# Expert weights in a ring of 16 places, loads of two places from the fifth expert on, put-back products in two groups of eight

## The reference

```python
def hier_moe(x, w_grp, b_grp, w_rt, b_rt, w_gate, w_up, w_down):
    ...
    gate = (one_hot(g_idx)[:, :, None] * within[:, None, :]).reshape(T, N_EXPERTS)
    h = silu(einsum("td,edf->tef", xt, w_gate)) * einsum("td,edf->tef", xt, w_up)
    y = einsum("tef,efd->td", h * gate[:, :, None], w_down)

def reference(...):
    h = x
    h = h + pool_mixer(rmsnorm(h, norm_mix[0]), pool_w[0], pool_scale[0])
    h = h + hier_moe(rmsnorm(h, norm_ffn[0]), ...)            # layer 0
    k, v = shared_kv(h, kv_norm, w_kv, k_norm)
    h = h + stick_breaking_layer(rmsnorm(h, norm_mix[1]), k, v, w_q[0], q_norm[0], w_o[0])
    return h + hier_moe(rmsnorm(h, norm_ffn[1]), ...)         # layer 1
```

## Time and profile before

| | us |
|---|---|
| Median of three runs | 1383.72 |
| The three runs | 1380.75, 1383.72, 1383.76 |
| The profiled execution, its time | 1382.63 |
| Its span (first to last instruction) | 1380.7 |
| PE busy | 1336.4 (97%) |
| DVE busy, ACT busy | 557.0 (40%), 412.3 (30%) |
| DMA moved | 480.86 MB, mean 348 GB/s |

### The profile page before, as it was taken

How to read it: one execution, slowest core, us unless ns; L and a number is a source line. 1 busy time by engine, 2 the same in 40 slices (tenths; PEclk the granted TensorE clock), 3 DMA queues, 4 the chain that set the end, 5 groups by cost and what they waited for, 6 DMA issues and landing times.

```text
span 1380.7 us, 21741 instructions
## 1 busy us (share of the span) xinstructions
PE 1336.4 (97%) x9081; PEld 761.2 (55%) x9081; DVE 557.0 (40%) x906; ACT 412.3 (30%) x636; POOL 45.6 (3%) x37
## 2 busy tenths in 40 slices
PE   9899999998999999999999999999999999899998
PEld 8544444443344458888888887764434444334443
DVE  5813223232222246666665665561323223122223
ACT  5611111110111136665656575541111111011112
POOL 2200000000000000000000000110000000000000
PEclk9999999999999999999999999999999999999999
DMA  9999999999999999654535545579999999999997
GB/s 358 420 412 421 420 420 421 425 427 428 428 426 425 421 393 374 196 165 160 182 125 189 173 152 183 182 279 376 420 421 420 422 425 426 429 428 427 424 421 287
DMA packets 86223, 480.86 MB, mean 348 GB/s; under 512 B 6402, under 2 KB 6612, under 8 KB 46972
## 3 DMA queue, kind: packets, MB, share of 16 engines
q1 hardware_dynamic: 85708, 476.98, 86.1%
q10 hardware_dynamic: 432, 2.65, 0.5%
HBM read 477.51 MB, written 2.10 MB: 347 GB/s over the span
## 4 chain that ended last, share of the span: by engine, by line
issue 53%; PE 35%; DMA 7%; DVE 2%; POOL 1%; ACT 1%; SPq 1%; POOLq 0%; DVEq 0%; ACTq 0%
PE ps L1833 12%; PE ps L1641 8%; DMA ring<-in_moe_w_up 6%; PE ps L1871 5%; PE ps L1722 2%; PE ps L1887 2%; PE ps L1798 1%; PE ps L1799 1%; POOL head_rs L669 1%; DMA bias_row<-in_moe_b_rt 1%; PE ps L1926 1%; PE ps L1860 0%; DVE ws L1068 0%; PE ps L1662 0%; PE ps L1939 0%
## 5 line engine op out<-in xcount | busy, mean ns | idle before, releaser
L1833 PE MATMUL ps<-ring,xg 128*64 128x512 f32 x1536 | 361.1, 600 | 24.6 <-DMA ring<-in_moe_w_up 19.4
L1641 PE MATMUL ps<-ws,xs 128*128 128x512 f32 x1632 | 382.2, 392 | 2.5 <-DVE ws L1071 1.1
L1641 PEld LDWEIGHTS ps<-ws,xs 128*128 128x128 f32 x1632 | 302.9, 188 | 70.4 <-DVE ws L1071 3.6
L1833 PEld LDWEIGHTS ps<-ring,xg 128*64 128x64 f32 x1536 | 115.1, 138 | 238.0 <-issue 237.7
L1871 PE MATMUL ps<-ring,hidT 128*64 128x512 f32 x800 | 177.3, 595 | 0.0
L1071 DVE SCALAR_TENSOR_TENSOR ws<-ring,vecs,ws 128x512 fp32r<-128x512 f32 x192 | 134.3, 747 | 87.5 <-ACT ws L690 87.5
L1265 DVE TENSOR_TENSOR y_lo<-ps,y_hi 64x512 fp32r<-64x512 f32 x112 | 77.1, 689 | 191.6 <-ACT y_hi L754 188.9
L690 ACT ACTIVATE ws<-ring,vecs 128x512 fp32r<-128x512 f32 x192 | 127.3, 716 | 83.2 <-PE ps L1641 83.1
L745 ACT ACTIVATE silu_g<-ps,slot_scale 64x512 f32<-64x512 f32 x28 | 19.1, 683 | 401.1 <-PE ps L1833 401.1
L1245 DVE TENSOR_TENSOR resid<-resid,ps 128x512 f32<-128x512 f32 x112 | 72.0, 684 | 165.0 <-PE ps L1799 165.0
L754 ACT ACTIVATE y_hi<-ps 64x512 fp32r<-64x512 f32 x112 | 66.2, 591 | 209.2 <-PE ps L1871 207.2
(11 more groups left out here) (201 smaller groups left out, 865.0 us busy)
## 6 DMA issues: line engine op xcount, KB each, us to landing
ring<-in_moe_w_down SPq DMA_DIRECT2D x68, 1024.0 KB, 16.6
ring<-in_moe_w_gate SPq DMA_DIRECT2D x64, 1024.0 KB, 15.9
ring<-in_moe_w_up SPq DMA_DIRECT2D x64, 1024.0 KB, 16.4
ring<-in_moe_w_gate SPq DMA_DIRECT2D x24, 2048.0 KB, 16.4
ring<-in_moe_w_up SPq DMA_DIRECT2D x24, 2048.0 KB, 20.6
ring<-in_moe_w_down SPq DMA_DIRECT2D x24, 2048.0 KB, 19.3
ring<-in_w_kv SPq DMA_DIRECT2D x32, 1024.0 KB, 5.4
ring<-in_w_q SPq DMA_DIRECT2D x16, 1024.0 KB, 5.2
```

The source lines that it names most:

```text
L1641: last = mm(ps[:, bank + t, :], xs[:, px, k, cols], ws[:, b, pw, j, :], start=(first and j == 0 and n == 0), stop=(last_unit and j == 1 an ...
L1833: last = mm(ps[CAP * h:CAP * h + CAP, b, :], xg[:, b, k, :], both[h][:, j, :], start=(k == 0), stop=(k == KD - 1))
```

## The change

- **Places.** Four `outer` places (the memory of four of the five `extra`) join the 12 of the ring, and all blocks go round these 16 to the end of the layer. The fifth extra, `spare`, is used for two blocks (block 11 of expert 0 and block 4 of expert 2), and the two early places once, as before. `stage_places` works out the place of each load and the value of `slot_read` from which it is free.
- **Loads.** Experts 0 to 3 are loaded block by block, and from expert 4 on a load carries two blocks. This takes in gate and up of experts 14 and 15 and down of 14; down of 15 stays in four column blocks. Where gate and up come in two-block loads, one load holds the gate weights of quarters 0 and 1, one the up weights of the same quarters. So the PE waits for both ahead of quarter 0 and for the other two ahead of quarter 2.
- **Release.** A load of two waits until both places are read. Blocks are reported read after quarter 1 (four) and quarter 3 (four).
- **Puts.** The four puts m = 0 to 3 (eight products) stand behind the second quarter and m = 4 to 7 behind the third. They write banks 2 to 5 in turn, m waits for addition m - 3, and the first put waits for all four low parts of the pair before. The down products of the even expert wait for six of the additions, because they write banks 2 and 3.
- **Loops.** PE's pairs 2 to 5 are a loop of two rounds with two pairs in each; SP's experts 4 to 11 are a loop of two rounds with four experts in each.

```diff
-PAIR_SLOTS = 2 * SLOTS
-EXTRA = 5
-EARLY = 2
-WIDE = SLOTS + EXTRA
-PEELED = 3
-AHEAD = PEELED * PAIR_SLOTS
...
+LOADS = SLOTS * EXP
+OUTER = 4
+SINGLES = 4
+SPARE, EARLY = SLOTS + OUTER, SLOTS + OUTER + 1
+LAST = EXP - 1
+ROUND = [[*range(4, SLOTS), *range(4), *range(SLOTS, SLOTS + OUTER)], [*range(8, SLOTS), *range(8), *range(SLOTS, SLOTS + OUTER)]]
+ONCE = {("one", 0, 6): EARLY, ("one", 0, 7): EARLY + 1, ("one", 0, 11): SPARE, ("one", 2, 4): SPARE}
+STAGE = ([("one", e, m) for e in range(SINGLES) for m in range(SLOTS)]
+         + [("two", e, m) for e in range(SINGLES, LAST - 1) for m in range(6)]
+         + [("two", e, m) for e in (LAST - 1, LAST) for m in range(4)]
+         + [("two", LAST - 1, m) for m in (4, 5)] + [("col", LAST, c) for c in range(NBLK)])
+def read_at(load):
+    kind, e, m = load
+    if kind == "one":
+        return SLOTS * e + (2 * (m // 2) + 2 if m < 8 else m + 1)
+    if kind == "col":
+        return LOADS - NBLK + m + 1
+    if e < LAST - 1:
+        return SLOTS * e + (4, 4, 8, 8, 10, 12)[m]
+    return SLOTS * (LAST - 1) + (8 if e == LAST or m > 3 else 0) + (4, 4, 8, 8, 10, 12)[m]
+def stage_places(l):
+    place_of, free_at, holds, at = {}, {}, {}, 0
+    for load in STAGE:
+        if load in ONCE:
+            taken = [ONCE[load]]
+        else:
+            n = 2 if load[0] == "two" else 1
+            taken, at = [ROUND[l][(at + j) % len(ROUND[l])] for j in range(n)], at + n
+        free_at[load] = max(holds.get(p, 0) for p in taken)
+        place_of[load] = taken[0]
+        for p in taken:
+            holds[p] = read_at(load)
+    return place_of, free_at, holds
...
-        extra = at(32 * KB, "extra", [P, EXTRA, 2048])
-        early = [at(16 * KB * j, f"early{j}", [P, 2048]) for j in range(EARLY)]
+        outer = at(32 * KB, "outer", [P, OUTER, 2048])
+        spare = at(64 * KB, "spare", [P, 2048])
+        early = [at(16 * KB * j, f"early{j}", [P, 2048]) for j in range(2)]
...
+        def DOUBLE_FREE(e, m):
+            return SLOTS * (e - 2) + (10, 12, 16, 16, 20, 20)[m]
...
-                        nc.vector.tensor_tensor(rb, rb, ps[:, 4 + t, :], ALU.add).then_inc(resid_added, 1)
+                        nc.vector.tensor_tensor(rb, rb, ps[:, 2 + m % 4, :], ALU.add).then_inc(resid_added, 1)
...
+                def doubles(e0, i=0):
+                    for e in range(e0, e0 + 4):
+                        for m in range(6):
+                            sp.wait_ge(slot_read, LOADS * l + DOUBLE_FREE(e, m) + SLOTS * 4 * i)
+                            expert_load(l, ("two", e, m), e + 4 * i)
+                with sp.Fori(0, 2) as i:
+                    doubles(SINGLES, i)
+                for one in STAGE[SLOTS * SINGLES + 6 * 8:]:
+                    sp.wait_ge(slot_read, LOADS * l + FREE_AT[l][one])
+                    expert_load(l, one, one[1])
...
+                def gate_up(e, q, s=None):
+                    if e < SINGLES:
+                        return [one_at(loaded(("one", e, 2 * q + h))).rearrange("p (k c) -> p k c", k=4) for h in range(2)]
+                    both = [("two", e, 2 * (q // 2) + h) for h in range(2)]
+                    if q % 2 == 0:
+                        for two in both:
+                            loaded(two, s)
+                    return [two_at(PLACE_OF[l][two]).rearrange("p a (j f) -> p (a j) f", j=4)[:, 4 * (q % 2):4 * (q % 2) + 4, :]
+                            for two in both]
+                def blocks_read(e, q):
+                    return 2 if e < SINGLES else 4 * (q % 2)
+                def down_weights(e, k, s=None):
+                    if e < SINGLES:
+                        return one_at(loaded(("one", e, 8 + k)))
+                    two = ("two", e, 4 + k // 2)
+                    if k % 2 == 0:
+                        loaded(two, s)
+                    return two_at(PLACE_OF[l][two])[:, k % 2, :]
...
-                    if t == 0:
-                        pe.wait_ge(y_lo_done, NBLK * ((EXP + 1) * l + 2 * i + 1) + c + 1)
-                    pe.wait_ge(resid_added, add0 + 8 * i + m - 1)
-                    mm(ps[:, 4 + t, :], putT[:, t * P:(t + 1) * P], y_hi[:, c, :], start=True, stop=False)
-                    mm(ps[:, 4 + t, :], putT[:, t * P:(t + 1) * P], y_lo[c], start=False, stop=True).then_inc(mix_done, 1)
+                    if m == 0:
+                        pe.wait_ge(y_lo_done, NBLK * ((EXP + 1) * l + 2 * i + 1) + NBLK)
+                    pe.wait_ge(resid_added, add0 + 8 * i + m - 3)
+                    mm(ps[:, 2 + m % 4, :], putT[:, t * P:(t + 1) * P], y_hi[:, c, :], start=True, stop=False)
+                    mm(ps[:, 2 + m % 4, :], putT[:, t * P:(t + 1) * P], y_lo[c], start=False, stop=True).then_inc(mix_done, 1)
+                def put_half(i, h):
+                    for m in range(4 * h, 4 * h + 4):
+                        put_rows(i, m)
...
-                            if b == 0 and before is not None:
-                                put_rows(before, 2 * q)
-                                put_rows(before, 2 * q + 1)
+                            if blocks_read(e, q):
+                                last.then_inc(slot_read, blocks_read(e, q))
+                            if b == 0 and before is not None and q in (1, 2):
+                                put_half(before, q - 1)
...
+                        elif before is not None:
+                            pe.wait_ge(resid_added, add0 + 8 * before + 6)
...
-                        put_rows(i - 1, 2 * q)
-                        put_rows(i - 1, 2 * q + 1)
+                        if q in (1, 2):
+                            put_half(i - 1, q - 1)
...
-                for i in range(1, PEELED):
-                    pair(i, i - 1)
-                with pe.Fori(PEELED, WIDE_FROM) as i:
-                    pair(i, i - 1, loop=PEELED)
-                with pe.Fori(WIDE_FROM, NPAIR - 2) as i:
-                    pair(i, i - 1, loop=WIDE_FROM)
+                pair(1, 0)
+                with pe.Fori(0, 2) as s:
+                    for first in (2, 3):
+                        pair(2 * s + first, 2 * s + first - 1, first, s)
```

243 lines of the change are left out of this document (88 added, 155 removed).

## The result

The changed kernel takes **1386.17 us** (median of 20, 1383.01 to 1388.85) where the kernel before takes 1383.51 us on the same chip (median of 20). The ratio is 1.0017, with a 95% interval of 1.0009 to 1.0024: slower by 2.3 us, where 3.1 us less was forecast, and outside the range. Measured again beside later experiments it was 1.0019 (1.0010 to 1.0027).

A forecast was written before the change was run, and what follows sets the result against it. The loads' stream was taken to bound each layer up to expert 13's third quarter, PE's work behind it. Per layer -2.0 + 0.75 - 0.3 = -1.55 us, twice -3.1, from 1383.72 gave 1380.6 us; range 1376.0 to 1385.5.

The forecast's parts named there:

- The loads of experts 4 to 13: Experts 4 to 7 go to two-block loads: 0.035 to 0.045 us less a block, 48 blocks, 2.0 us a layer.
- D: Start of expert 13's third quarter, end of PE's last wait for up weights in a layer; forecast 2.0 us earlier.
- rival 3: A smoother stream: fewer, larger loads may avoid irregular losses, 2.2 us in layer 0; 1378.4 us; chance 0.15.
- The last pair's doubles: Two-block loads make expert 14's first and third quarters wait for more blocks, giving back about 0.75 us a layer.
- D': The instant D as forecast for the changed kernel, 2.0 us earlier.
- cap at expert 15's third quarter: It needs 20 blocks, D' + 49.0; PE arrives at D' + 49.2, so at most 0.2 us more comes through.
- The puts: Expert 14's third quarter to the gather takes 9.10 us instead of 9.41, 0.3 us less a layer.
- Places: Sixteen places instead of twelve only let loads be issued earlier; a longer queue moves nothing while DMA share is 1.01.
- 1 (slow clock in the last pair): Rival: the new wait at expert 14's first quarter sets off slow clock, +1.0 us a layer; 1382.6 us; chance 0.15.
- 2: Rival: the load stream runs dry at experts 4 to 7, two-block loads freed too late; 1392.6 us; chance 0.08.
- 4: Rival: PE is the bound after all, the puts count in all seven pairs, 9.1 us; 1374.6 us; chance 0.03.
- 5: Rival: the fixed cost per load is real, savings cut to PE's 24.6 us of waits; 1359 us; chance 0.01.

The follow-up runs named there:

- Run 4: Kernel before with experts 6 and 7 also in two-block loads, PE's pairs 3 to 5 as one loop of three rounds: 1379.22 us, 0.9978.
- Run 9: Kernel after with experts 14 and 15 in single loads, 12 places from expert 6 on, pairs 3 to 5 one loop of one-pair rounds: 1377.30 us, 0.9960.
- run 3: Kernel before with only the puts changed, to two groups of eight as in the kernel after: 1382.47 us, 0.9997.
- run 1: Kernel before with PE's loops over expert pairs written out: 1383.87 us, 1.0005.
- run 2: Kernel after with PE's loop of two rounds of two pairs written out, so no branch back: 1383.44 us, 1.0005.
- run 6: Kernel after with experts 14 and 15 in single-block loads, all else kept: 1380.67 us, 0.9982.
- run 10: Run 9 with experts 14 and 15 in two-block loads as in the kernel after: 1382.40 us, 0.9991.
- run 12: Kernel after, unchanged, measured once more: 1386.11 us, 1.0019.
- run 7: Kernel after, 16 places kept, but each two-block load from expert 4 on issued only as in a ring of 12: 1398.76 us, 1.0114.
- run 13: Run 9 with expert 14's gate and up in two-block loads: 1380.43 us, 0.9981.
- run 14: Run 9 with expert 15's gate and up in two-block loads: 1385.35 us, 1.0016.
- run 11: Run 6 (last pair in single loads) with PE's loop of two pairs written out: 1378.56 us, 0.9969.

## Why the prediction was wrong, step by step

**The loads of experts 4 to 13: right.** 427 GB/s from expert 4 on. Run 4 puts a price on it: with the 6 packets fewer taken off (1.1 us by the price above), it gained 1.9 us for 24 blocks a layer, 0.04 us a block as forecast. Run 9's 5.5 us can then be shared out as 3.8 of doubles, 1.1 of fetches and 0.6 of puts; this is an estimate, no run has the parts alone.

**D: 2.0 us a layer forecast.** From a layer's start it came 1.5 and 0.2 us earlier (0.7 earlier and 0.3 later in the second execution). The sum did not hold the 6 more fetches a layer, about 1.1 us at the price above. The rest is within what single executions scatter: in layer 1 the one profile of before has 370.66 us, where its loads took 371.40 and 371.91 in runs 3 and 1. The branch back doesn't delay D (run 2), but with its 4 packets it costs about 1.8 us of the time. Both are a step left out, put at nothing without a reason, and not a size missed: the section on the change treated the loop of two pairs as a mere rewriting. It was there to see. The prediction found that pair 5 took 58.74 us and pair 6 60.27, and put the irregular 1.5 us down as something that larger loads might avoid (rival 3). The queue of TensorE's instructions in the kernel before shows 1 packet from 315 to 374 us (pair 5, the loop's second round) and 4 from 374 to 434 us (pair 6, code not run before). At 0.18 us each these 3 are about 0.5 of the 1.5 us.

**The last pair's doubles: 0.75 us a layer forecast, 2.2 to 2.5 measured (runs 6 and 10).** The instants were nearly right: third quarter of expert 14 at D' + 29.4 (29.4 to 30.4 in four layers of two executions), cap at expert 15's third quarter at D' + 49.0 (49.6 to 50.4). The failing step is what these were held against, "before, this start was D + 28.65". That figure held 1.7 us of slow clock, as the prediction itself said one sentence earlier. At the full clock the singles get there at D + 26.57, and with the low clock and the new puts at 28.3 (461.66 - 433.40 in run 6). So the doubles cost 1.1 us at the low clock and 2.8 at the full one, at expert 14 alone. The slow clock isn't all of the miss. At the low clock the new puts bring the singles to the third quarter 0.4 us sooner (28.3 instead of 28.65), which the doubles' wait swallows and the sum didn't count. By expert 15's fourth quarter the doubles are 1.6 us behind even where D was at the low clock in both (D + 54.27 in run 12, 52.64 in run 6). Then the cap, worked out as 0.2 us away, was taken as harmless; without doubles there is no cap at 49, since expert 15's third quarter needs six of its blocks and not all eight.

**The puts: right.** From the third quarter to the gather 473.79 - 464.68 = 9.11 us, 9.10 forecast, 9.41 before.

**Places: right in the sense meant, wrong in the word "only".** Nothing points to harm or gain from the longer queue in itself: run 9, which has 12 places again from expert 6 on, came out where its sum without such an effect had it. But with 12 places at expert 4 the stream would have run dry for 6 to 7 us a layer (run 7).

**Attention, start of layer 1: right.** The start of layer 0's experts was 1.0 us late (63.52 against 62.50), behind products at the low clock; the same code started between 61.1 and 64.0 in the other kernels, so this belongs to the execution. So does about 1 us in the final stores: from the last put product to the end of the span 5.9 us in the profile before, 7.1 after, and 5.7 to 7.7 in the others.

**Rivals.** 1 (slow clock in the last pair) did not come in the kernel after: its products last 7.09 and 3.65 us. It came in runs 13 and 14. The low clock came at expert 8, behind the branch's wait (8.83 us for 32 products). 2 did not come, by the margin of four buffers. 3, 4 and 5 are out: nothing got faster by their sizes, and the stream got no smoother (the slice around 90 us shows 389 GB/s, where it was 412).

**The sum again**, in us against before, from the ratios: kernel after without branch and without the last pair's doubles -4.3 (run 11; forecast for the rest of the change -4.6, in which the 8 more fetches, 1.5, did not stand); the last pair's doubles +4.9 (forecast +1.5); the branch back with 4 fetches +1.8 (forecast 0). Together +2.4; measured +2.3 and +2.6. These terms are differences along one chain of kernels (run 11, run 6, the kernel after), so that they add up to the measured +2.3 says nothing by itself. Terms from other runs test it: -4.3, with 4.3 for the doubles (run 10) and 1.7 for the branch (run 2), gives +1.7, which agrees within the uncertainty. Of the 5.4 us between forecast and result 3.4 are thus the last pair's doubles, and 1.8 the branch with its packets; the puts and the other loads, with 1.5 us of fetches against them, came out within 0.3 us of their -4.6.

## What to carry to other kernels

Where a stream of loads and an engine take turns in setting the pace, merge loads only where the engine has blocks in hand, and leave the last stretch, behind the last wait, in small pieces: the merged loads cost 2.2 to 2.5 us a layer here, against the 0.04 us a block that they gain. When a load's form forces a longer loop body, read the queue of the engine's instructions in a window of the loop's second round, in the kernel before and, where it can be had, after. And when a start is compared with one read from the trace, take the slow clock out of both or out of neither.
